# Cross-attention: products of the output projection placed inside the attention, on one pair of output banks

## What is computed

```python
def memory_cross_attention(h, mem_n, wq, wkv, wo):
    q = (h @ wq).reshape(bsz, seq, XA_HEADS, XA_DIM)      # 4 heads of 256
    k, v = jnp.split(mem_n @ wkv, 2, axis=-1)             # 256 memory rows
    ...
    s = jnp.einsum('bshd,bmhd->bhsm', q, k).astype(jnp.float32) * (XA_DIM ** -0.5)
    p = jax.nn.softmax(s, axis=-1).astype(v.dtype)
    o = jnp.einsum('bhsm,bmhd->bshd', p, v).reshape(bsz, seq, D_MODEL)
    return o @ wo
```

## Time and profile before

| what | us |
|---|---|
| median of 3 runs (3687.59, 3687.77, 3699.86) | 3687.77 |
| the profiled execution, its own time | 3688.61 |
| its span, first to last instruction | 3686.8 |
| PE busy | 3543.5 (96%) |
| DVE busy | 2031.8 (55%) |
| POOL busy | 1928.7 (52%) |
| ACT busy | 1003.1 (27%) |
| mean granted clock of PE, as a share of full speed | 0.981 |

### The profile page before, as it was taken

The page is one execution under the profiler, slowest core; times in us unless marked ns, Lnnn a source line. Parts: engine busy times, 40 slices in busy tenths (PEclk is TensorE's granted clock), DMA queues, the critical chain, the costliest instruction groups (busy, mean ns, idle before and its releaser), DMA issues.

```text
span 3686.8 us, 44206 instructions
## 1 busy us (share of the span) xinstructions
PE 3543.5 (96%) x16768; PEld 2891.0 (78%) x16768; DVE 2031.8 (55%) x2964; ACT 1003.1 (27%) x1662; POOL 1928.7 (52%) x1177
## 2 busy tenths in 40 slices
PE   8999998989999999999898999999999999999998
PEld 6888776878888888877687888877778887777877
DVE  5553597636552454269663654256666526766641
ACT  2121246232110111024623211024433203533310
POOL 5666451436666666645143666642266663246664
PEclk9999998999999999999899999999999999999999
DMA  3233281312233322338141223344122335412222
GB/s 133 97 93 94 90 189 48 120 53 97 97 95 94 98 97 95 100 100 190 30 132 49 95 97 94 100 141 115 41 92 97 94 101 146 109 56 92 97 87 86
DMA packets 106684, 362.43 MB, mean 98 GB/s; under 512 B 14304, under 2 KB 14720, under 8 KB 105856
## 3 DMA queue, kind: packets, MB, share of 16 engines
q1 hardware_dynamic: 91648, 319.41, 27.2%
q0 software_dynamic: 8640, 31.46, 4.6%
q10 hardware_dynamic: 6208, 8.92, 0.9%
HBM read 317.27 MB, written 2.10 MB: 87 GB/s over the span
## 4 chain that ended last, share of the span: by engine, by line
PE 71%; DVE 14%; issue 6%; ACT 6%; DMA 2%; POOL 1%; ACTq 1%; DVEq 0%; SPq 0%; POOLq 0%
PE banks L556 23%; PE banks L557 23%; PE banks L558 23%; DVE diagonals L934 2%; DMA w_raw<-mid 1%; DVE h_lo L916 1%; ACT probs L997 1%; DVE squares L938 1%; DVE square_sum L680 1%; DVE conv_acc L1622 1%; DVE bias L1597 1%; DVE diagonals L1622 1%; DVE best L1593 1%; ACT diagonals L903 1%; ACT probs L991 1%
## 5 line engine op out<-in xcount | busy, mean ns | idle before, releaser
L592 POOL CAST w_hi<-w_raw 128x1024 fp32r<-128x1024 f32 (+1 forms) x540 | 563.4, 1043 | 1390.3 <-PE banks L558 1308.0
L597 POOL TENSOR_TENSOR w_lo<-w_raw,w_hi 128x1024 fp32r<-128x1024 f32 (+1 forms) x508 | 1234.9, 2431 | 40.7
L556 PE MATMUL banks<-h_hi,w_hi 128*128 128x512 f32 x2928 | 1160.5, 396 | 41.9 <-DVE h_lo L916 13.7
L557 PE MATMUL banks<-h_lo,w_hi 128*128 128x512 f32 x2928 | 1146.9, 392 | 0.0
L558 PE MATMUL banks<-h_hi,w_lo 128*128 128x512 f32 x2928 | 1146.5, 392 | 0.0
L556 PEld LDWEIGHTS banks<-h_hi,w_hi 128*128 128x128 f32 x2928 | 553.9, 189 | 176.8 <-issue 39.7
L558 PEld LDWEIGHTS banks<-h_hi,w_lo 128*128 128x128 f32 x2928 | 553.6, 189 | 117.0
L557 PEld LDWEIGHTS banks<-h_lo,w_hi 128*128 128x128 f32 x2928 | 554.4, 189 | 110.9
L556 PE MATMUL banks<-act_hi,w_hi 128*128 128x512 f32 x1056 | 412.2, 390 | 5.2 <-DVE act_lo L944 4.2
L557 PE MATMUL banks<-act_lo,w_hi 128*128 128x512 f32 x1056 | 411.7, 390 | 0.0
L558 PE MATMUL banks<-act_hi,w_lo 128*128 128x512 f32 x1056 | 411.7, 390 | 0.0
(11 more groups left out here) (412 smaller groups left out, 4422.0 us busy)
## 6 DMA issues: line engine op xcount, KB each, us to landing
w_raw<-gu SPq DMA_DIRECT2D x176, 512.0 KB, 3.5
w_raw<-mid SPq DMA_DIRECT2D x120, 512.0 KB, 3.5
w_raw<-up SPq DMA_DIRECT2D x88, 512.0 KB, 3.4
w_raw<-dn SPq DMA_DIRECT2D x96, 448.0 KB, 3.3
w_raw<-mix SPq DMA_DIRECT2D x62, 512.0 KB, 3.5
w_lo<-w_raw POOLq DMA_DIRECT2D x50, 512.0 KB, 5.1
w_raw<-dn SPq DMA_DIRECT2D x48, 512.0 KB, 3.5
w_raw_third<-mid SPq DMA_DIRECT2D x10, 512.0 KB, 5.7
```

The source lines that it names most:

```text
L556: pe.matmul(out, w_hi, m_hi, start=start, stop=False, skip_group_check=True)
L557: pe.matmul(out, w_hi, m_lo, start=False, stop=False, skip_group_check=True)
L592: g.tensor_copy(wh[:, ch.slot, 0:width], raw_tile(ch, width)).then_inc(Ring.hi[ch.slot], 1)
L597: eng.tensor_tensor(wl[:, ch.slot, 0:width], raw_tile(ch, width), f32(wh[:, ch.slot, 0:width]), ALU.subtract).then_inc(Ring.split[ch.slot], 1)
```

## The change

A function wo_bank(d) gives projection tile d one of four banks, 6, 7, 0, 1 by turns. All heads' outputs now go to banks 4 and 5, so that the outputs of a head wait for the low parts of the head before (out_banks is 1). A projection tile can now be made in parts, by heads: out_heads(d, h, end) issues the products of tile d with the output tiles of heads h to end - 1, behind a wait for their low parts. The function beside(s), called where `between` stands in PE's step, issues tiles 0 and 1 for head 0 at steps 10 and 11, for head 1 at steps 14 and 15, for head 2 at steps 18 and 19. Behind the outputs of the last head PE issues tile 2 for heads 0 to 2, then tiles 0, 1 and 2 for head 3, then tiles 3 to 7 whole. The lines for ACT and DVE change only in their banks.

```diff
--- before.py
+++ after.py
@@ -1103,6 +1103,10 @@
 
         return mid_chunk(l, MEMK_CHUNK + i)
 
+    def wo_bank(d):
+
+        return bank[(6, 7, 0, 1)[d % 4]]
+
     def part_at(d):
 
         return 8 + 7 * d // 2
@@ -1360,18 +1364,36 @@
             for e in range(2):
                 feats = slice((2 * h + e) * P, (2 * h + e + 1) * P)
                 for j in range(MT):
-                    mm = mm3(pe, bank[4 + 2 * (h % 2) + e][:, :], vm_hi[:, j, feats], vm_lo[:, j, feats],
+                    mm = mm3(pe, bank[4 + e][:, :], vm_hi[:, j, feats], vm_lo[:, j, feats],
                              xpt_hi[h % 2][:, j, :], xpt_lo[h % 2][:, j, :], j == 0, j == MT - 1)
             return mm
 
-        attention_pe(pe, xat, l, scores, XSCORE_BANKS, xat.exp, lambda t: MT, outputs, xat.y_lo)
-        pe.wait_ge(xat.y_lo.sem, xat.y_lo(l, 2 * XH))
-        for d in range(KD):
+        def out_heads(d, h, end):
             ch = mid_chunk(l, XO_CHUNK + d)
-            landed(pe, ch)
-            pe.wait_ge(wo_x.sem, wo_x(l, d - 1))
-            column_tile(pe, ch, bank[d % 2][:, :], KD, lambda k: qx_hi[:, k, :], lambda k: qx_lo[:, k, :])\
-                .then_inc(Ring.done, 1)
+            if h == 0:
+                landed(pe, ch)
+            pe.wait_ge(xat.y_lo.sem, xat.y_lo(l, 2 * end))
+            for k in range(2 * h, 2 * end):
+                b = k * P
+                mm = mm3(pe, wo_bank(d)[:, :], wh[:, ch.slot, b:b + P], wl[:, ch.slot, b:b + P], qx_hi[:, k, :],
+                         qx_lo[:, k, :], k == 0, k == KD - 1)
+            if end == XH:
+                mm.then_inc(Ring.done, 1)
+
+        def beside(s):
+            for h in range(XH - 1):
+                for d in range(2):
+                    if s == T * h + T + AHEAD + LAG + 2 + d:
+                        out_heads(d, h, h + 1)
+
+        attention_pe(pe, xat, l, scores, XSCORE_BANKS, xat.exp, lambda t: MT, outputs, xat.y_lo, beside, 1)
+        pe.wait_ge(xat.exp.sem, xat.exp(l, xat.items))
+        out_heads(2, 0, XH - 1)
+        for d in range(3):
+            out_heads(d, XH - 1, XH)
+        for d in range(3, KD):
+            pe.wait_ge(wo_x.sem, wo_x(l, d - 3))
+            out_heads(d, 0, XH)
 
     def mix1_act(act, l):
         plain_act(act, mixnorm, l, lambda k: par1_at(l, 1, k), lambda a, k: a.wait_ge(ffn1.x.sem, ffn1.x(l, k + 1)))
@@ -1500,7 +1522,7 @@
 
         def out_hi(h):
             for e in range(2):
-                act.activation(qx_hi[:, 2 * h + e, :], bank[4 + 2 * (h % 2) + e][:, :], ACT.Copy)\
+                act.activation(qx_hi[:, 2 * h + e, :], bank[4 + e][:, :], ACT.Copy)\
                     .then_inc(xat.y_hi.sem, 1)
 
         attention_act(act, xat, l, XSCORE_BANKS, lambda t: MT, xpt_hi, out_hi)
@@ -1734,14 +1756,14 @@
         def out_lo(h):
             for e in range(2):
                 v.wait_ge(xat.y_hi.sem, xat.y_hi(l, 2 * h + e + 1))
-                v.tensor_tensor(qx_lo[:, 2 * h + e, :], bank[4 + 2 * (h % 2) + e][:, :], f32(qx_hi[:, 2 * h + e, :]),
+                v.tensor_tensor(qx_lo[:, 2 * h + e, :], bank[4 + e][:, :], f32(qx_hi[:, 2 * h + e, :]),
                                 ALU.subtract).then_inc(xat.y_lo.sem, 1)
 
         attention_dve(v, xat, l, XSCORE_BANKS, None, lambda t: MT, xpt_hi, xpt_lo, out_lo)
 
         def add_cross(d):
             products_done(v, mid_chunk(l, XO_CHUNK + d))
-            v.tensor_tensor(x[:, d, :], x[:, d, :], bank[d % 2][:, :], ALU.add).then_inc(wo_x.sem, 1)
+            v.tensor_tensor(x[:, d, :], x[:, d, :], wo_bank(d)[:, :], ALU.add).then_inc(wo_x.sem, 1)
 
         add_tiles(v, add_cross, ffn2norm, l, lambda k: plain_low(v, ffn2norm, l, lambda d: par1_at(l, 4, d), k))
```

## The result

| | before | changed |
|---|---|---|
| median, 20 runs each | 3690.44 us (3680.36 to 3699.86) | 3700.27 us (3692.10 to 3703.86) |
| ratio of changed to before | | 1.0022, 95% interval 1.0015 to 1.0029 |
| span of the profiled execution | 3686.8 us | 3695.1 us |

The change makes the kernel slower by 8 us (5.5 to 10.7), a fifth of a per cent. In a second session the ratio was 1.0018 (1.0005 to 1.0030).

The account below looks back on a forecast made before the run. TensorE (PE), busy 96%, bounds the kernel; a loop of ACT and DVE paces the attention. Order -3.2 us plus clock +6.0 gave +2.8 on 3688.61, 3691.4, less 0.84 for the median: 3690.5 us, range 3682 to 3698.

Parts of the forecast that it names:

- the count of low stretches: Stretches of 3.4 us at 1.2 GHz, not 2.4; four taken to follow the changed kernel's six long waits.
- PE's place in its order: In the attention, each head's first block waits for low parts with transposes queued behind; head periods near 12, 11.5, 8.5 us.
- The last wait covered, and the fourth tile late: After the last outputs the third tile covers PE's 2.0 us wait; the fourth tile stalls 1.15 us for POOL's split.
- The banks cost nothing: Output banks 4 and 5 alone add no wait; four projection banks, not two, only ease waits for the additions.
- The sum at equal clock: Attention start to fourth tile: layer 0 at 829.35 against 830.37, -1.0 us; layer 1 -2.2; sum -3.2 if clock high.
- Four of six at 1.5, +6.0: Clock loss behind the three long waits per layer: four of six followed by 1.2 GHz at 1.5 us; bounds 0, +10.2.
- The anchor: The profiled execution's 3688.61 us less 0.84 for the median of the runs shown, the base of the forecast sum.
- the clock falling after each wait: Rival, 0.17: low clock after all six waits at blocks, 1.7 us each, +7, 3694.8; 3697 with a longer signal chain.

Follow-up runs that it names:

- run without the wait: The changed kernel with its six blocks inside the attention reading the normed hidden state, ready long before; ratio to before 0.9944 (0.9924 to 0.9963).
- run with later blocks: The changed kernel, blocks of heads 0 and 1 three steps later behind the transposes, head 2's behind the last outputs, no third tile ahead; ratio to before 0.9953.
- filled kernel before: The kernel before with 8 and 7 useless matmuls in its last two waits; ratio to before 0.9997 (0.9984 to 1.0010).

## Why the prediction was right or wrong

It named the mechanism and missed the size: 3700.27 us lies outside 3682 to 3698. Within half a per cent of before was right. The step that failed is the count of low stretches: four in the changed kernel against the three of before's profiled execution, one more, where the clocks of all executions show 3.8 more.

- **PE's place in its order.** Right, almost to the tenth. The first block was worked out for 792.3, or 789.35 with the shift of 2.95, and stands at 789.35. The periods were 12.5, 11.6 and 8.5; where no low clock falls, they are 12.6, 11.8 and 8.7. The run without the wait shows that it is the wait and not the work, the run with later blocks that the same order of work can hide it.
- **The last wait covered, and the fourth tile late.** Right: no wait before the third tile, 1.02 us for POOL where 1.15 was worked out. (The working's own terms, 825.45 + 3.5 + 0.25, give 829.2 and a wait of 1.0; 829.35 is a slip.) Leaving the third tile out brings the wait of 2.1 back, taking one tile for three takes the late split away.
- **The banks cost nothing.** Right as far as 0.9999 (0.9988 to 1.0009) tells.
- **The sum at equal clock** was 57.65 us for a stage (829.35 less 771.70); it is 58.03. Short by 0.4 per layer, 0.8 in all; the periods are longer than worked out by 0.1 to 0.2 each, which is all of it.
- **The clock, the term that failed.** "Four of six at 1.5, +6.0", 3.0 per layer. The three profiled executions have 62.35 - 58.03 = 4.3 per layer. The price of one was right (1.4 to 1.5), the number was not: I counted waits, each followed by one stretch or none, but low stretches also came two in a row, and one (1972.8) fell early in the attention, where PE has no long wait. There were four or five in four of the six layers and one in the other two. That is 2.6 us in all. Against it, the kernel before also loses more than its one profiled execution shows, 119.5 us for two stages on the mean of four and not 118.5.
- Together by the stages: forecast +2.8 us; the stages give 2 x (62.35 - 59.75) = +5.2, of it 1.9 order and 3.3 clock. That is 0.3 below the interval of the time, 5.5 to 10.7, with six and four stages that scatter by 2 us each. Span less both stages is 3571.9, 3573.3 and 3568.4 us in the changed kernel, 3568.3 and 3573.5 in the one before, too much scatter to find 3 us in.
- **The clocks of all executions** close most of that gap. At half speed the changed kernel spends 158.4 us on the mean of 33 executions, the kernel before 145.5 on the mean of 75, all of the later sessions: 12.9 us more, which is 3.8 low stretches (standard error 0.5), where the stages of the profiled executions had 2.8. At 1.4 to 1.5 each they cost 5.3 to 5.7 us, with the 1.9 of the order 7.2 to 7.6, inside the interval. (A straight line through the times and clocks of all executions, each kernel with its own level, gives some 1.1 us per low stretch; by that price the sum is 6.1, inside it too.) My sum had one more low stretch (1.6 us over before's three) and 1.2 for the order. These clocks do not tell where in the kernel the low stretches fall.
- **The anchor.** I set the sum on a median of three runs, 3687.77; with twenty it is 3690.44. 2.7 us of the 9.8 by which the forecast missed are this, 0.8 the order, and some 4 the clock. Of the 2.3 left, 1.7 is that the two medians differ by 9.8 and the ratio gives 8.1. A range that took the scatter of the three runs shown (12 us) more seriously would have held the time.

Of the rivals, the one that came nearest is the clock falling after each wait (3694.8 to 3697, 0.17). The Trainium skill, in "TensorE: Matmul & The Clock Gate" (HAM oscillation, how this bites in real kernels), tells of a kernel whose PE waited for data ahead of each slice, longer than PE waits here, and was throttled anew every time. The trace agrees in part, with waits of 3.1, 3.0 and 2.3 us: in the layers with four low stretches or more all three waits have one beside them, in the layers with 59.5 only the second has, and the longest, of 3.1 us, has none.

## What to carry to other kernels

An engine that runs ahead of the others in a software pipeline has idle time, but not at the step where the others produce what the new work needs: at that step of its own count it is still ahead, and everything behind the new wait pays. Put the filling work as many steps later as the engine is ahead (here three), behind what the others wait for, and it can be free, as it was here. Three steps is the one distance that was tried, and with it the third tile went and head 2's blocks moved behind the outputs; the side of the transposes and the third tile were each tried alone, and the first gives a part of it (7 us of 24) and the second none. Look at PE's waits of 2 to 3 us twice, for themselves and for the half-speed stretch that may follow. And price a change of 0.2% in a clock that falls differently in each execution by the clocks of all executions and not by one profiled execution: the six layers of the changed kernel showed from one low stretch to five.

## What I had not expected of the hardware

33 useless matmuls per layer, 7.5 us of PE work at 0.2267 each, made the kernel faster by about 14 us against the same order without them, with the granted clock at 1.00 in both stages (ratios to before 0.9984, 0.9970 to 0.9997, and 1.0022, 1.0015 to 1.0029). And waits as short as 1.69 us were followed by a stretch at 1.2 GHz (in the filled kernel before, at 799.1), while one of 3.11 us in the changed kernel's layer 0 (789.35) was not, and a stretch fell at 781.7 in the run without the wait, where PE had been idle for 0.44 us at the most.
